# Prompt attention: probabilities, unnormalised and split in two, as the weights of the value product

## The chip, the core and the metric

The kernel runs on one core of a Trainium2 chip. The metric is the time of one launch on the device, in microseconds (us); lower is better. Before the change it is 2110.23 us, the median of three runs (2109.89 to 2110.86). Engines are named as the profile names them: PE is the matmul engine (TensorE), PEld its weight loads, DVE the vector engine, ACT the scalar engine, POOL is GpSimd, SP issues the DMAs.

## The reference

One layer of a hybrid decoder: a combined input projection, latent attention on one side and a gated convolution on the other, one output projection, and an MLP. It treats 1040 prompt tokens (16 learned ones and 1024 of the prompt) and 8 sampled sequences of 4 tokens with a paged cache. Only the attention of the prompt among itself matters here: 8 heads, queries and keys of 96 elements, values of 64.

```python
def block(args):
    qblk, i = args
    qpos = i * Q_BLOCK + jnp.arange(Q_BLOCK)
    s = jnp.einsum('bqhd,bkhd->bhqk', qblk, k).astype(jnp.float32) * ATTN_SCALE
    s = jnp.where(kpos[None, :] <= qpos[:, None], s, -jnp.inf)
    p = jax.nn.softmax(s, axis=-1).astype(v.dtype)
    return jnp.einsum('bhqk,bkhd->bqhd', p, v)
```

Everything is fp32. Where the kernel wants fp32 accuracy from the cheaper matmul on rounded fp32 (type F32R in the code), it splits an operand into a rounded high part and the rest, the low part, and adds three products: high by high, high by low, low by high.

## The kernel before

Six stages run one after the other, with a barrier of all engines behind each: inputs, prompt attention, sampled attention, output projection, MLP, stores. Every engine's program is written out by hand, in order, with semaphores between the engines; there is no scheduler. Only the function `prompt_attention` changes.

It works head by head (`head(n, par, ...)`): head 0, a loop over pairs of heads, head 7. A head has nine blocks of 128 queries, t = 0 to 8 (NT = 9). The last one holds only 16 real tokens of the prompt (1040 = 8 * 128 + 16); the 32 sampled tokens and zeros fill it up. Block t attends to keys 0 to (t + 1) * 128, so it has t + 1 key blocks.

- `transpose_unit` (PE), `split_hi` (ACT), `split_lo` (DVE) turn the next head's queries and keys, four blocks at a time, and split them: five units, in steps t = 1 to 5 of the head before, through bank 5.
- `score` (PE) writes the scores of block t + 2 in step t, queries as weights, keys as the moving side, three products of rounded parts; the mask is added by a matmul of bf16.
- `maxima` (DVE) takes the row maxima of block t + 2 and turns their sign; `probabilities` (ACT) computes the exponentials of block t + 1 and their row sums.
- DVE inverts the row sums of block t and scales its probabilities by them, in place (line 1159).
- PE turns the scaled probabilities with fp32 transposes, in jobs of up to four key blocks ("chunks", at most 512 columns) through the one bank 6 (line 1228). ACT copies each chunk to SBUF (`probsT`, line 1106).
- `values` (PE, line 1204) multiplies, in plain fp32, each key block's values (128 keys x 64, the weights) by the turned probabilities (128 keys x 128 queries, the moving side) and adds up over the key blocks in bank 7. The product of a chunk is issued behind the transposes of the next one. Its result is already values by queries, the form that the output projection wants; ACT copies it to `attnT` (line 1087).

So the order on PE in step t is: scores of t + 2, a unit of the next head, chunk 0 of t, values of the last chunk of t - 1, chunk 1 of t, values of chunk 0 of t, and so on. Every engine takes its instructions strictly in this written order. POOL scales each head's queries, keys and values ahead of time.

Of the kernel before, what the change touches and what calls it, by code (L numbers as in the profile page):

```python
# [971 lines left out]
def prompt_attention(g):  # L972
# [10 lines left out]
    pt = [ar.take(f"probsT{i}", [P, 4, P], F32) for i in range(2)]  # L983
# [4 lines left out]
    vh = [ar.take(f"v_head{i}", [P, NT, VH], F32) for i in range(2)]  # L988
# [4 lines left out]
        "ready gain_done q_head_ready k_head_ready v_head_ready unit_transposed unit_hi_done unit_lo_done scored "  # L993
        "maxed biased exped inverted normed p_transposed p_copied pv_done out_copied").split()}
# [4 lines left out]
    UNIT_BANK = 5  # L999

    SCORE_BANK = (0, 1, 2, 0, 3, 0, 3, 0, 2)
    SCORE_FREE = (-1, -1, 0, 1, 0, 4, 5, 6, 7)

    def chunks(t):
        return [(j, min(4, t + 1 - j)) for j in range(0, t + 1, 4)]
# [6 lines left out]

    def score_shape(t):
        pieces = -(-(t + 1) * P // BANK)
        return pieces, (t + 1) * P // pieces

    def scores(t):
        pieces, n = score_shape(t)
        return banks[:, SCORE_BANK[t]:SCORE_BANK[t] + pieces, 0:n]
# [9 lines left out]
    with nc.Block() as block:  # L1029
        @block.gpsimd  # L1030
        def _(pool):
# [7 lines left out]
            def prepare(n, par):  # L1039
                scale = lambda r, c: r[:, :, ds(n, 1)].broadcast_to([P, NT, c])  # L1040
                pool.wait_ge(s["unit_transposed"], LEAD + n * NU)
# [3 lines left out]
                nc.gpsimd.tensor_mul(kh[:, :, NOPE:QK], g.kpe_tok[:, :, :], scale(g.rk, ROPE)).then_inc(s["k_head_ready"], 1)  # L1045
                if not isinstance(n, int) or n > 1:
                    pool.wait_ge(s["pv_done"], LEAD + n * NCH - NCH)
                nc.gpsimd.tensor_mul(vh[par][:, :, :], g.v_tok[:, :, ds(n * VH, VH)],
                                     g.inv_kv[:, 0:NT].unsqueeze(2).broadcast_to([P, NT, VH])).then_inc(s["v_head_ready"], 1)
# [10 lines left out]
        def _(act):  # L1060
            act.sem_inc(s["exped"], LEAD)
            act.sem_inc(s["p_copied"], LEAD)
            act.sem_inc(s["out_copied"], LEAD)
            act.wait_ge(s["gain_done"], 1)

            def split_hi(n, par, u, bank=UNIT_BANK):
                act.wait_ge(s["unit_transposed"], LEAD + n * NU + (u + 1))
                for queries, t, m, place in UNITS[u]:
                    src = banks[0:QK, bank, place * P:(place + m) * P]
                    if queries:  # L1070
                        act.activation(q_hi[par][0:QK, t * P:(t + m) * P], src, ACT.Copy, scale=g.gg[0:QK, :])\
                            .then_inc(s["unit_hi_done"], 1)
                    else:
                        act.copy(k_hi[par][0:QK, t * P:(t + m) * P], src).then_inc(s["unit_hi_done"], 1)

            def probabilities(n, par, t):
                m = (t + 1) * P
                pieces, L = score_shape(t)
                act.wait_ge(s["biased"], n * NT + (t + 1))
                act.wait_ge(s["p_transposed"], LEAD + n * NCH + before(t - 1))  # L1080
                act.activation(probs[(par + t) % 2][:, 0:m].rearrange("p (a b) -> p a b", a=pieces), scores(t), ACT.Exp,
                               bias=nb[:, t:t + 1], scale=SCALE, accum_out=rs[:, t:t + 1]).then_inc(s["exped"], 1)

            def keep_output(n, par, t):
                act.wait_ge(s["pv_done"], LEAD + n * NCH + before(t + 1))
                w = min(P, TP - t * P)
                act.copy(g.attnT[VH * par:VH * par + VH, ds(n // 2, 1), t * P:t * P + w]
                                      .rearrange("p o t -> p (o t)"), banks[0:VH, 7, 0:w]).then_inc(s["out_copied"], 1)

            def head(n, par, first, last):  # L1090
                if first:
                    for u in range(NU):
                        split_hi(0, 0, u, u)
                    probabilities(0, 0, 0)
                c = 0
                for t in range(NT):
                    if t + 1 < NT:
                        probabilities(n, par, t + 1)
                    elif not last:
                        probabilities(n + 1, 1 - par, 0)  # L1100
                    if not last and 1 <= t <= NU:
                        split_hi(n + 1, 1 - par, t - 1)
                    for j, m in chunks(t):
                        act.wait_ge(s["p_transposed"], LEAD + n * NCH + (c + 1))
                        act.wait_ge(s["pv_done"], LEAD + n * NCH + (c - 1))
                        act.copy(pt[(par + c) % 2][:, 0:m, :], banks[:, 6, 0:m * P].rearrange("p (j q) -> p j q", q=P))\
                            .then_inc(s["p_copied"], 1)
                        c += 1
                        if j == 0 and t >= 1:
                            keep_output(n, par, t - 1)  # L1110
                        elif j == 0 and not first:
                            keep_output(n - 1, 1 - par, NT - 1)
                if last:
                    keep_output(n, par, NT - 1)
# [4 lines left out]
        def _(v):  # L1119
            v.sem_inc(s["unit_lo_done"], LEAD)  # L1120
# [3 lines left out]
            def split_lo(n, par, u, bank=UNIT_BANK):  # L1124
                last = u == NU - 1
                v.wait_ge(s["unit_hi_done"], n * (NU + 1) + (u + 1 + last))
# [8 lines left out]
                if last:  # L1135
                    at = TP - (NT - 1) * P
                    nc.vector.tensor_scalar(g.qs[0:QK, ds(n, 1), :].rearrange("p o t -> p (o t)"), banks[0:QK, bank, at:at + NS],
                                            g.gg[0:QK, :], None, ALU.mult).then_inc(s["unit_lo_done"], 1)
                else:
# [1009 lines left out]
```

## Time and profile before

| | |
|---|---|
| median of three runs | 2110.23 us |
| the profiled execution's own time | 2108.73 us |
| its span, first to last instruction | 2107.0 us |
| prompt attention in it | from 335 to 597 us: 262 us |
| of these, PE busy, granted clock | 251.08 us, 0.97 |
| of these, DVE, ACT, POOL busy | 148.13, 154.96, 39.45 us |
| one head in steady state | 31.47 us |

The timeline names each instruction's start, its duration, engine, line, operation, output and inputs, and the shape; "x8" at the end merges eight of a kind in a row. A plain fp32 matmul appears as two records, a matmul on rounded fp32 as one. A matmul's duration holds its way through the array, and matmuls overlap: what one costs is the distance from one start to the next, which for a merged row of x8 is the duration less that of one (0.27 us at 128 columns), divided by 7. A busy PE in the table is therefore not a PE without stalls.

### The profile page before, as it was taken

How to read it: one execution, taken by the hardware profiler on the slowest of the kernel's cores; microseconds unless marked ns; L12 is line 12 of the kernel's file. 1: busy time of each engine (PE TensorE's matmuls, PEld its weight loads, DVE VectorE, ACT ScalarE, POOL GpSimd, SP SyncE). 2: the span in 40 equal slices, each digit the busy share in tenths (PEclk: the TensorE clock that was granted, in tenths of full speed). 3: DMA queues.
4: the chain of work that ended last, by engine and by line, in shares of the span. 5: the costliest groups of instructions: out<-in, count | busy, mean ns of one | idle time of the engine just before them, and what ended most of it. 6: DMA issues, size and time to landing. Idle time of an engine off the chain costs nothing. (4 is left out here: it accounts for less than half of the span.)

```text
span 2107.0 us, 38039 instructions
## 1 busy us (share of the span) xinstructions
PE 2002.8 (95%) x13358; PEld 1877.5 (89%) x13358; DVE 928.2 (44%) x1679; ACT 796.6 (38%) x1702; POOL 428.4 (20%) x391
## 2 busy tenths in 40 slices
PE   6999997999969999999999698899999999999998
PEld 5999985777749999999998496799999999999998
DVE  6125145556536777777777622521222222221222
ACT  5012134656635666666666311311121111212121
POOL 3233133111010000010000323331222222231221
PEclk7999998999979999999999598899999999999999
DMA  6122000000022222222222111020202011120202
GB/s 213 50 64 63 10 19 9 1 1 0 0 71 63 77 74 73 70 75 73 74 69 107 40 40 29 22 61 26 75 15 65 25 55 50 30 61 24 75 15 97
DMA packets 180599, 108.42 MB, mean 51 GB/s; under 512 B 52132, under 2 KB 177154, under 8 KB 180276
## 3 DMA queue, kind: packets, MB, share of 16 engines
q1 hardware_dynamic: 180358, 107.21, 17.7%
q8 instruction: 44, 0.72, 0.1%
q10 hardware_dynamic: 174, 0.30, 0.1%
q14 instruction: 23, 0.19, 0.0%
HBM read 97.47 MB, written 10.00 MB: 51 GB/s over the span
## 5 line engine op out<-in xcount | busy, mean ns | idle before, releaser
L1750 PE MATMUL banks<-comb_hi,pageT_hi 128*128 128x272 f32 x1024 | 234.3, 310 | 0.0
L1640 DVE TENSOR_REDUCE k_sums<-k_sq 128x8 f32<-128x512 f32 x256 | 174.4, 681 | 92.3 <-ACT k_sq L1462 92.3
L1750 PE MATMUL banks<-comb_hi,pageT_lo 128*128 128x272 f32 x1024 | 212.5, 289 | 0.0
L1750 PE MATMUL banks<-comb_lo,pageT_hi 128*128 128x272 f32 x1024 | 212.2, 289 | 0.0
L1462 ACT ACTIVATE k_sq<-banks 128x512 f32<-128x512 f32 x256 | 152.0, 594 | 142.4 <-PE banks L1750 139.4
L2045 DVE TENSOR_TENSOR xT<-xT,banks 128x1074 f32<-128x1074 f32 x64 | 81.5, 1274 | 277.4 <-PE banks L244 277.4
L2035 DVE TENSOR_TENSOR relu_squared<-relu 128x1074 f32<-128x1074 f32 x32 | 40.9, 1278 | 305.2 <-ACT relu L1949 305.2
L1949 ACT ACTIVATE relu<-banks 128x1074 f32<-128x1074 f32 x32 | 34.3, 1071 | 360.3 <-PE banks L244 351.9
L244 PE MATMUL banks<-a_hi,w_down_hi 128*128 128x358 f32 x768 | 168.2, 327 | 0.0
L244 PE MATMUL banks<-a_hi,w_down_lo 128*128 128x358 f32 x768 | 167.7, 326 | 0.0
L244 PE MATMUL banks<-a_lo,w_down_hi 128*128 128x358 f32 x768 | 167.6, 326 | 0.0
L233 POOL TENSOR_TENSOR w_down_lo<-w_down_raw,w_down_hi 128x512 fp32r<-128x512 f32 x64 | 94.7, 1479 | 348.0 <-ACT w_down_hi L229 348.0
L1750 PEld LDWEIGHTS banks<-comb_lo,pageT_hi 128*128 128x128 f32 x1024 | 161.8, 189 | 0.0
L1750 PEld LDWEIGHTS banks<-comb_hi,pageT_lo 128*128 128x128 f32 x1024 | 161.0, 190 | 0.0
L1750 PEld LDWEIGHTS banks<-comb_hi,pageT_hi 128*128 128x128 f32 x1024 | 158.1, 191 | 0.0
L244 PE MATMUL banks<-hf_hi,w_up_lo 128*128 128x358 f32 x720 | 157.5, 327 | 0.0
L244 PE MATMUL banks<-hf_hi,w_up_hi 128*128 128x358 f32 x720 | 157.0, 326 | 0.3 <-POOL w_up_lo L233 0.3
L244 PE MATMUL banks<-hf_lo,w_up_hi 128*128 128x358 f32 x720 | 157.1, 326 | 0.0
L244 PEld LDWEIGHTS banks<-a_hi,w_down_hi 128*128 128x128 f32 x768 | 133.3, 189 | 0.0
L244 PEld LDWEIGHTS banks<-a_hi,w_down_lo 128*128 128x128 f32 x768 | 132.8, 189 | 0.0
L244 PEld LDWEIGHTS banks<-a_lo,w_down_hi 128*128 128x128 f32 x768 | 131.6, 189 | 0.0
L229 ACT CAST w_down_hi<-w_down_raw 128x512 fp32r<-128x512 f32 x64 | 39.5, 617 | 237.4 <-PE banks L244 237.4
(371 smaller groups left out, 4044.3 us busy)
## 6 DMA issues: line engine op xcount, KB each, us to landing
page_latents<-in_cache_kv_latent SPq DMA_DIRECT2D x256, 128.0 KB, 2.1
w_up_raw<-in_w_up SPq DMA_DIRECT2D x32, 512.0 KB, 4.2
w_down_raw<-in_w_down SPq DMA_DIRECT2D x64, 256.0 KB, 2.8
w_in_raw<-in_w_in SPq DMA_DIRECT2D x17, 512.0 KB, 3.8
x_spill<-xT SPq DMA_DIRECT2D x1, 4296.0 KB, 13.9
xT<-x_spill SPq DMA_DIRECT2D x1, 4296.0 KB, 12.8
page_ropes<-in_cache_k_rope SPq DMA_DIRECT2D x256, 16.0 KB, 1.8
w_o_raw<-in_w_o SPq DMA_DIRECT2D x8, 512.0 KB, 4.2
```

The source lines that it names most:

```text
L229: act.copy(self.hi[s][:, :, :], self.raw[s][:, :, :]).then_inc(self.hi_done[s], 1)
L233: nc.gpsimd.tensor_sub(self.lo[s][:, :, :], self.raw[s][:, :, :], self.hi[s][:, :, :].bitcast(F32)).then_inc(self.lo_done[s], 1)
L244: mm = pe.matmul(out[:, b, 0:TB], w[s][:, k, :], x(k)[:, b * TB:(b + 1) * TB], start=k == 0 and a == 0, stop=k == self.K - 1 and a == 2)
L1462: act.activation(sq[j % 2][:, :].rearrange("p (a c) -> p a c", a=2), kn[:, :, 0:WK], ACT.Square)\
L1640: nc.vector.tensor_reduce(ksum[par][:, j, :], sq[j % 2][:, :].rearrange("p (h c) -> p h c", h=H), AX_X, ALU.add)\
L1750: mm = pe.matmul(banks[:, 2 * (j % 2) + half, 0:WC], x[j % AHEAD][:, k, :], w[par][:, k, half, :], start=k == 0 and a == 0, stop=k == KL - ...
L1949: act.activation(relu[:, f % 2, :].rearrange("p (b t) -> p b t", b=NBLK), banks[:, 3 * (f % 2):3 * (f % 2) + 3, 0:TB], ACT.Relu)\
L2035: nc.vector.tensor_mul(full[:, s, :], relu[:, s, :], relu[:, s, :]).then_inc(sq_done, 1)
L2045: nc.vector.tensor_add(x, x, banks[:, 3 * s:3 * s + 3, 0:TB]).then_inc(down.evacuated[s], 1)
```

## The change

The exponentials are no longer scaled. PE turns them as they are; ACT writes their rounded high part (`probsT_hi`) and DVE the rest (`probsT_lo`). The value product changes sides: the turned probabilities (128 keys x 128 queries) are the weights, the values the moving side. POOL splits the values too, into one tile of 128 columns, 64 high and 64 low. Each key block takes two matmuls on rounded fp32: the high probabilities by all 128 columns, the low probabilities by the 64 high ones. The result has queries on the partitions and two halves; ACT scales the low half by the inverse row sum (`scale_low`), DVE scales the high half and adds the low one (`keep_output`), into `out_tokens`. Behind the last head, PE turns all of `out_tokens`, 36 transposes in nine groups, and ACT and DVE copy the groups to `attnT` in turns.

The units and the chunks share two banks, 5 and 6, in turns: a job may start when the last but one is split. Block 8 works on its 16 real rows only, turns its nine key blocks in one job of 16 columns each, and the values of that job are issued behind the scores of block 2 of the next head.

```diff
-    pt = [ar.take(f"probsT{i}", [P, 4, P], F32) for i in range(2)]
+    pt_hi, pt_lo = ([ar.take(f"{n}{i}", [P, 4, P], F32R) for i in range(2)] for n in ("probsT_hi", "probsT_lo"))
...
-    vh = [ar.take(f"v_head{i}", [P, NT, VH], F32) for i in range(2)]
+    vf = ar.take("v_head", [P, NT, VH], F32)
+    vh = [ar.take(f"v_head_split{i}", [P, NT, 2 * VH], F32R) for i in range(2)]
+    part = [ar.take(f"out_low{i}", [P, VH], F32) for i in range(2)]
+    out_tok = ar.take("out_tokens", [P, NT, AW], F32)
...
-        return [(j, min(4, t + 1 - j)) for j in range(0, t + 1, 4)]
+        return [(j, min(4, t + 1 - j)) for j in range(0, t + 1, 4)] if t < LAST else [(0, NT)]
...
+    def job_bank(n, par, at):
+        return 5 + (at + par * NJ) % 2
...
     def score_shape(t):
+        if t == LAST:
+            return 3, 352
...
             def prepare(n, par):
...
+                nc.gpsimd.tensor_mul(vh[par][:, :, 0:VH], g.v_tok[:, :, ds(n * VH, VH)],
+                                     g.inv_kv[:, 0:NT].unsqueeze(2).broadcast_to([P, NT, VH])).then_inc(s["v_high"], 1)
...
+                nc.gpsimd.tensor_sub(vh[par][:, :, VH:2 * VH], vf[:, :, :], vh[par][:, :, 0:VH].bitcast(F32))\
+                    .then_inc(s["v_head_ready"], 1)
...
+            def scale_low(n, t, scaled):
+
                 act.wait_ge(s["pv_done"], LEAD + n * NCH + before(t + 1))
...
+                act.activation(part[scaled % 2][0:rows(t), :], banks[0:rows(t), OUT_BANK, VH:2 * VH], ACT.Copy,
+                               scale=ri[0:rows(t), t:t + 1]).then_inc(s["out_scaled"], 1)
...
                     for j, m in chunks(t):
-                        act.wait_ge(s["p_transposed"], LEAD + n * NCH + (c + 1))
+                        job = job_of_chunk(n, t, c, last)
+                        act.wait_ge(s["turned"], LEAD + job + 1)
                         act.wait_ge(s["pv_done"], LEAD + n * NCH + (c - 1))
-                        act.copy(pt[(par + c) % 2][:, 0:m, :], banks[:, 6, 0:m * P].rearrange("p (j q) -> p j q", q=P))\
-                            .then_inc(s["p_copied"], 1)
+                        act.copy(split_keys(pt_hi[(par + c) % 2], t, m), turned_keys(job_bank(n, par, in_head(t, c, last)), t, m))\
+                            .then_inc(s["hi_done"], 1)
...
+            def keep_output(n, t, scaled):
+                v.wait_ge(s["out_scaled"], LEAD + n * NT + (t + 1))
+                nc.vector.scalar_tensor_tensor(out_tok[0:rows(t), t, ds(n * VH, VH)], banks[0:rows(t), OUT_BANK, 0:VH], ri[0:rows(t), t:t + 1],
+                                               part[scaled % 2][0:rows(t), :], ALU.mult, ALU.add).then_inc(s["out_done"], 1)
...
                 for t in range(NT):
                     v.wait_ge(s["exped"], LEAD + n * NT + (t + 1))
-                    nc.vector.reciprocal(ri[:, t:t + 1], rs[:, t:t + 1]).then_inc(s["inverted"], 1)
-                    v.wait_ge(s["inverted"], n * NT + (t + 1))
-                    pr = probs[(par + t) % 2][:, 0:(t + 1) * P]
-                    nc.vector.tensor_scalar(pr, pr, ri[:, t:t + 1], None, ALU.mult).then_inc(s["normed"], 1)
+                    nc.vector.reciprocal(ri[0:rows(t), t:t + 1], rs[0:rows(t), t:t + 1]).then_inc(s["inverted"], 1)
                     if t + 2 < NT:
-                        maxima(n, par, t + 2)
+                        maxima(n, t + 2)
...
+                    for j, m in chunks(t):
+                        v.wait_ge(s["hi_done"], LEAD + job_of_chunk(n, t, c, last) + 1)
+                        nc.vector.tensor_sub(split_keys(pt_lo[(par + c) % 2], t, m),
+                                             turned_keys(job_bank(n, par, in_head(t, c, last)), t, m),
+                                             split_keys(pt_hi[(par + c) % 2], t, m).bitcast(F32)).then_inc(s["split"], 1)
+                        c += 1
+                        if j == 0 and t >= 1:
+                            keep_output(n, t - 1, par + t - 1)
...
-                pe.wait_ge(s["p_copied"], LEAD + n * NCH + (c + 1))
+                pe.wait_ge(s["split"], LEAD + job_of_chunk(n, t, c, last) + 1)
                 if j == 0:
-                    pe.wait_ge(s["out_copied"], LEAD + n * NT + t)
+                    pe.wait_ge(s["out_done"], LEAD + n * NT + t)
+                hi, lo = split_keys(pt_hi[(par + c) % 2], t, m), split_keys(pt_lo[(par + c) % 2], t, m)
                 for x in range(m):
-                    mm = pe.matmul(banks[0:VH, 7, 0:P], vh[par][:, j + x, :], pt[(par + c) % 2][:, x, :],
-                                   start=j + x == 0, stop=j + x == t)
+                    k = slice(0, rows(j + x))
+                    pe.matmul(banks[0:rows(t), OUT_BANK, 0:2 * VH], hi[k, x, :], vh[par][k, j + x, :], start=j + x == 0, stop=False)
+                    mm = pe.matmul(banks[0:rows(t), OUT_BANK, 0:VH], lo[k, x, :], vh[par][k, j + x, 0:VH], start=False, stop=j + x == t)
                 mm.then_inc(s["pv_done"], 1)
...
                     for j, m in chunks(t):
-                        pe.wait_ge(s["p_copied"], LEAD + n * NCH + c)
+                        job, bank = job_of_chunk(n, t, c, last), job_bank(n, par, in_head(t, c, last))
+                        pe.wait_ge(s["split"], LEAD + job - 1)
+                        if t == LAST:
+                            values(*behind)
+                            behind = None
...
+                if last:
+                    values(*behind)
+                    for t in range(NT):
+                        pe.wait_ge(s["out_done"], LEAD + n * NT + (t + 1))
...
+                        for k in range(AW // P):
+                            mm = pe.transpose(banks[:, t % 4, k * P:k * P + rows(t)], out_tok[0:rows(t), t, k * P:(k + 1) * P],
+                                              ident[0:rows(t), 0:rows(t)])
+                        mm.then_inc(s["out_turned"], 1)
```

How the written order moves, at two places. In the rows a name's number tells buffers apart; REGISTER_ALU and ISA rows prepare a wait's value in the loop over heads. First DVE, from block 5's step on, before: the sums inverted, the probabilities scaled, then the maxima of block 7 and the last unit's split.

```order
L1156 RECIPROCAL row_inv<-row_sum 128x1
L1159 TENSOR_SCALAR probs_2934<-probs_2934,row_inv 128x768
L1144 TENSOR_REDUCE row_max<-banks 128x1
L1146 TENSOR_SCALAR neg_max<-row_max 128x1
L1126 REGISTER_ALU
L1131 SCALAR_TENSOR_TENSOR q_lo_2918<-banks,qk_gain,q_hi_2916 96x128
L1134 TENSOR_TENSOR k_lo_2922<-banks,k_hi_2920 96x128
L1137 ISA
L1137 TENSOR_SCALAR q_sampled<-banks,qk_gain 96x32
L1155 REGISTER_ALU
L1156 RECIPROCAL row_inv<-row_sum 128x1
L1159 TENSOR_SCALAR probs_2935<-probs_2935,row_inv 128x896
```

The same step now, from the maxima of block 7 on.

```order
L1202 TENSOR_REDUCE row_max<-banks 128x1
L1204 TENSOR_SCALAR neg_max<-row_max 128x1
L1183 REGISTER_ALU
L1185 REGISTER_ALU
L1190 SCALAR_TENSOR_TENSOR q_lo_2918<-banks,qk_gain,q_hi_2916 96x128
L1193 TENSOR_TENSOR k_lo_2922<-banks,k_hi_2920 96x128
L1196 ISA
L1196 TENSOR_SCALAR q_sampled<-banks,qk_gain 96x32
L1229 REGISTER_ALU
L1230 TENSOR_TENSOR probsT_lo_2927<-banks,probsT_hi_2925 128x512
L1208 ISA
L1208 SCALAR_TENSOR_TENSOR out_tokens<-banks,row_inv,out_low_2942 128x64
```

The scaling is gone, and behind the maxima and the unit's split stand two new steps that PE waits for: the low parts of block 5's chunk of 512 columns (`probsT_lo`) and the sum of an output block (`out_tokens`).

Second PE, at the end of a head, before: block 8's three chunks, each followed by the values of the one ahead of it, then the scores of the next head's block 2.

```order
L1204 MATMUL banks<-probsT_2924,v_head_2937 64x128 x4
L1226 REGISTER_ALU
L1228 MATMUL banks<-ident,probs_2935 128x128 x4
L1202 REGISTER_ALU
L1204 MATMUL banks<-probsT_2925,v_head_2937 64x128 x4
L1226 REGISTER_ALU
L1228 MATMUL banks<-ident,probs_2935 128x128
L1204 MATMUL banks<-probsT_2924,v_head_2937 64x128 x4
L1200 REGISTER_ALU
L1204 MATMUL banks<-probsT_2925,v_head_2937 64x128
L1190 REGISTER_ALU
L1195 MATMUL banks<-k_hi_2920,q_hi_2916 128x384
```

The same place now: block 8's one job, then the scores of the next head's block 2, its first chunk, and the first of block 8's value products.

```order
L1318 MATMUL banks<-ident,probs_2937 128x16 x8
L1318 MATMUL banks<-ident,probs_2937 16x16
L1269 REGISTER_ALU
L1276 MATMUL banks<-k_hi_2920,q_hi_2916 128x384
L1276 MATMUL banks<-k_lo_2922,q_hi_2916 128x384
L1274 MATMUL banks<-causal_mask,ident_bf_2929 128x128
L1276 MATMUL banks<-k_hi_2920,q_lo_2918 128x384
L1307 REGISTER_ALU
L1312 ISA
L1318 MATMUL banks<-ident,probs_2936 128x128
L1281 REGISTER_ALU
L1287 MATMUL banks<-v_head_split_2940,probsT_hi_2925 16x128
```

Three chunks became one with 16 columns a key block, and its values moved behind the scores and the first chunk of the next head.

## Rows read from the trace of the kernel before

**Rows 1.** Windows view, one steady head: us, busy of PE, PEld, DVE, ACT, POOL; clock.
```profile
core 0: us, PE busy (x) PEld busy (x) DVE busy (x) ACT busy (x) POOL busy (x), PEclk, DMA share, GB/s
425.88:457.35 31.47, 30.77 (x210) 23.80 (x207) 18.74 (x44) 19.33 (x49) 4.95 (x5) 1.00 0.00 1
```

**Rows 2.** Groups by shape, attention stage: busy us, mean ns, idle before and its enders.
```profile
L1228 PE MATMUL banks<-ident,probs 128*128 128x128 f32 x360 | 62.7, 283 | 3.7 <-ACT probsT L1106 2.5 <-DVE probs L1159 0.4
L1134 DVE TENSOR_TENSOR k_lo<-banks,k_hi 96x512 fp32r<-96x512 f32 x16 | 11.0, 685 | 0.2 <-ACT k_hi L1074 0.2
```

**Rows 3.** Timeline, PE, starts around blocks 4 to 8: start, duration, instruction, tiles, count.
```profile
425.29 0.27 PE L1182 MATMUL banks<-ident,q_head 128*96 128x128 f32 x1
...
428.17 0.44 PE L1195 MATMUL banks<-k_hi,q_hi 96*128 96x384 f32 x1
...
429.99 0.60 PE L1228 MATMUL banks<-ident,probs 128*128 128x128 f32 x4
...
431.27 0.55 PE L1228 MATMUL banks<-ident,probs 128*128 128x128 f32 x3
...
432.76 0.33 PE L1195 MATMUL banks<-k_hi,q_hi 96*128 96x128 f32 x1
...
433.23 0.62 PE L1228 MATMUL banks<-ident,probs 128*128 128x128 f32 x4
...
436.18 0.38 PE L1195 MATMUL banks<-k_hi,q_hi 96*128 96x256 f32 x1
...
436.77 0.60 PE L1228 MATMUL banks<-ident,probs 128*128 128x128 f32 x4
...
441.42 0.44 PE L1195 MATMUL banks<-k_hi,q_hi 96*128 96x384 f32 x1
...
451.55 0.60 PE L1182 MATMUL banks<-ident,k_head 128*96 128x128 f32 x4
...
455.12 0.50 PE L1195 MATMUL banks<-k_hi,q_hi 96*128 96x512 f32 x1
```

**Rows 4.** Timeline, DVE, the maxima and what starts behind them.
```profile
425.49 1.23 DVE L1144 TENSOR_REDUCE row_max<-banks 128x1 f32<-128x1024 f32 x1 [2.57 <-PE banks L1195]
...
427.47 0.15 DVE L1156 RECIPROCAL row_inv<-row_sum 128x1 f32<-128x1 f32 x1
...
430.19 1.36 DVE L1144 TENSOR_REDUCE row_max<-banks 128x1 f32<-128x1152 f32 x1 [1.05 <-PE banks L1195]
...
431.58 0.15 DVE L1146 TENSOR_SCALAR neg_max<-row_max 128x1 f32<-128x1 f32 x1
...
451.75 1.09 DVE L1144 TENSOR_REDUCE row_max<-banks 128x1 f32<-128x896 f32 x1 [0.80 <-PE banks L1195]
...
453.58 0.15 DVE L1156 RECIPROCAL row_inv<-row_sum 128x1 f32<-128x1 f32 x1
```

**Rows 5.** Timeline, ACT, one copy of turned probabilities.
```profile
430.63 0.58 ACT L1106 COPY probsT<-banks 128x512 f32<-128x512 f32 x1 [1.89 <-PE banks L1228]
```

**Rows 6.** Timeline, PE and PEld: prices of matmuls and of weight loads.
```profile
263.00 2.36 PEld L894 LDWEIGHTS banks<-ones,lora_squares 128*128 128x128 f32 x20
...
432.93 0.28 PE L1195 MATMUL banks<-k_lo,q_hi 96*128 96x128 f32 x1
...
433.04 0.23 PE L1194 MATMUL banks<-causal_mask,ident_bf 128*128 128x128 bf16 x1
...
433.08 0.31 PE L1195 MATMUL banks<-k_hi,q_lo 96*128 96x128 f32 x1
...
435.18 1.08 PE L1204 MATMUL banks<-probsT,v_head 128*64 128x128 f32 x8
```

**Rows 7.** Groups by shape, weight loads of rounded fp32 in the sampled stage.
```profile
L1750 PEld LDWEIGHTS banks<-comb_hi,pageT_lo 128*128 128x128 f32 x1024 | 161.0, 190 | 0.0
```

**Rows 8.** Timeline, the end of the attention stage.
```profile
594.80 1.31 PE L1204 MATMUL banks<-probsT,v_head 128*64 128x128 f32 x10
...
596.14 0.16 ACT L1087 COPY attnT<-banks 64x16 f32<-64x16 f32 x1 [0.97 <-PE banks L1204]
```

More of the change, by code:

```diff
@@ L1079, in probabilities @@
+                    done.then_inc(s["hi_done"] if i == len(UNITS[u]) - 1 else s["unit_hi"], 1)
+            def probabilities(n, t):
+                m = score_shape(t)[0] * score_shape(t)[1]
                 act.wait_ge(s["biased"], n * NT + (t + 1))
[L1080 to L1082 removed]
@@ L1092, in head @@
                     for u in range(NU):
[L1093 to L1094 removed]
+                        unit_high(0, u, u, u)
+                    parity["par"] = 0
+                    probabilities(0, 0)
                 c = 0
@@ L1097, in head @@
                     if t + 1 < NT:
-                        probabilities(n, par, t + 1)
-                    elif not last:
-                        probabilities(n + 1, 1 - par, 0)
-                    if not last and 1 <= t <= NU:
-                        split_hi(n + 1, 1 - par, t - 1)
+                        parity["par"] = par
+                        if t >= 1:
+                            act.wait_ge(s["turned"], LEAD + job_of_chunk(n, t - 1, before(t) - 1, last) + 1)
+                        elif not first:
+                            act.wait_ge(s["turned"], LEAD + job_of_chunk(n - 1, LAST, NCH - 1, False) + 1)
@@ L1103, in head @@
+                        probabilities(n, t + 1)
+                    elif not last:
+                        parity["par"] = 1 - par
+                        act.wait_ge(s["turned"], LEAD + job_of_chunk(n, t - 1, before(t) - 1, last) + 1)
+                        probabilities(n + 1, 0)
+                    if not last and UNIT_AT(t) is not None:
+                        u = UNIT_AT(t)
+                        unit_high(1 - par, u, job_bank(n, par, before(t) + u), job_of_unit(n, u))
                     for j, m in chunks(t):
-                        act.wait_ge(s["p_transposed"], LEAD + n * NCH + (c + 1))
+                        job = job_of_chunk(n, t, c, last)
+                        act.wait_ge(s["turned"], LEAD + job + 1)
@@ L1164, in head @@
-                    if not last and 1 <= t <= NU:
-                        split_lo(n + 1, 1 - par, t - 1)
+                        maxima(n + 1, t + 2 - NT)
+                    if not last and UNIT_AT(t) is not None:
+                        u = UNIT_AT(t)
+                        unit_low(n + 1, 1 - par, u, job_bank(n, par, before(t) + u), job_of_unit(n, u))
+                    for j, m in chunks(t):
[6 more added lines that the diff above has]
+                            keep_output(n, t - 1, par + t - 1)
+                        elif j == 0 and not first:
+                            keep_output(n - 1, LAST, 1 - par + LAST)
@@ L1167, in _ @@
+                if last:
+                    keep_output(n, LAST, par + LAST)
+                    for t in range(1, NT, 2):
+                        v.wait_ge(s["out_turned"], t + 1)
+                        nc.vector.tensor_copy(g.attnT[:, :, t * P:t * P + rows(t)],
+                                              banks[:, t % 4, :].rearrange("p (k q) -> p k q", q=P)[:, :, 0:rows(t)])\
+                            .then_inc(s["out_copied_dve"], 1)
             heads(v, head)
```

166 lines of the change are left out of this document (98 added, 68 removed).

## Prediction

> **What bounds the kernel now.** I read the windows view first, for the stage and one head in it, then the timeline of that head on PE and on DVE side by side, then the waits and single prices. The change lives in the prompt attention alone, 262 of 2107 us. In a steady head PE is busy for 30.77 of 31.47 us while DVE and ACT are busy for 18.74 and 19.33 and POOL for 4.95 [rows 1]. So PE bounds the stage, and the clock is full (1.00) all through the head. But a busy PE holds short waits: the matmuls' ends reach over the next start. What counts is the distance between starts. The reader is to see in [rows 3] the five stretches between the end of one block's scores and the start of the next block's scores, in which the value path runs. I name them by the block t whose probabilities are turned there: t=4 from 451.55 to 455.12, 3.57 us; t=5 from 425.29 to 428.17, 2.88; t=6 from 429.99 to 432.76, 2.77; t=7 from 433.23 to 436.18, 2.95; t=8 from 436.77 to 441.42, 4.65. Wherever PE must wait for another engine in the new order, the stretch grows, however cheap its matmuls became.
>
> **Prices.** A turn of one key block costs (0.60 - 0.27) / 3 = 0.11 us [rows 3]. A value product before: eight records, four products, start 435.18, next scores 436.18, so 1.00 us for four, of which (1.08 - 0.27) / 7 = 0.116 a record or 0.232 a product, and 0.07 us for the change of group [rows 3, 6]. From the end of a turn to ACT's copy pass 0.04 us, the copy of 512 columns takes 0.58, and PE starts 0.06 us behind it (430.59, 430.63, 431.21, 431.27) [rows 3, 5]. The new split on DVE is the operation that splits keys now: 512 columns out of PSUM, 0.69 us [rows 2].
>
> The new product takes two matmuls per key block. The first, 128 rounded columns behind a fresh load of 128 weight columns, is of the shape of block 0's scores: from 432.93 to 433.04, 0.11 us [rows 6]. The second, 64 columns, is in no row. Its load is: twenty loads of 128 fp32 columns for matmuls of only 2 columns came (2.36 - 0.19) / 19 = 0.114 us apart, so a load that nothing hides sets the pace at 0.114 [rows 6], and a load of rounded fp32 has the same duration, 190 ns against 0.19 us [rows 6, 7]. I take 0.11 + 0.112 = 0.222 us a pair. Bounds: 0.15 if the second matmul costs what the mask's bf16 matmul does (433.04 to 433.08, 0.04), 0.34 if no load runs ahead of its matmul, as for the first of a group (432.76 to 432.93, 0.17) [rows 3, 6]; the stream of twenty is the nearest row, since there too each matmul brings its load. So 0.232 becomes 0.222: the weights are twice as wide now, and a product still loads twice.
>
> [...]
>
> **The steps, one steady head.** DVE takes its work in the written order, and the new split of chunk 0 of block t stands behind the maxima of block t + 2, which wait for the scores that PE has just finished. Behind PE's wait for that split stand the values, then the next scores, so all of it is on the path. Time counts from the start of the stretch.
> - t=4: DVE starts the maxima at 0.20, and what stands behind them and the unit's split starts at 453.58 - 451.55 = 2.03 [rows 3, 4]. There the split goes: 2.03 + 0.69 + 0.06 = 2.78 until PE goes on, then four pairs, 4 x 0.222 + 0.07 = 0.96: 3.74 against 3.57, +0.17.
> - t=5: 427.47 - 425.29 = 2.18 until the unit's parts are done [rows 3, 4], + 0.69 + 0.06 + 0.96 = 3.89 against 2.88, +1.01. This is the largest wait: PE has only 1.2 us of other work there.
> - t=6: the maxima of block 8 end with the sign change at 431.58 - 429.99 = 1.59 [rows 3, 4]; 96 columns fewer take 0.10 off (1.36 against 1.23 us for 128), the sign change 0.15: 1.64 + 0.69 + 0.06 + 0.96 = 3.35 against 2.77, +0.58.
> - t=7: the maxima are short; turn and copy decide: 0.64 + 0.58 + 0.04 + 0.69 + 0.06 + 0.96 = 2.97 against 2.95, +0.02.
> - t=8: four pairs 0.96 and one turn of nine key blocks with 16 columns. No row has that shape; between 0.04 and 0.11 I take 0.06 each, 0.61 in all. Block 8's nine pairs have 16 weight columns, so the matmuls decide: 0.11 for 128 columns and half of it for 64, 9 x 0.17 + 0.07 = 1.60 (bounds 0.08 and 0.22 a pair). They run behind the next scores, which hide their split. 3.17 against 4.65, -1.48.
> - Scores of block 8: 32 of 384 columns less, 1.82 us (428.17 to 429.99) x 32 / 384 = -0.15. Blocks 0 to 2: six pairs, -0.06.
>
> Sum: +0.09 us a head. PE's work falls by about 2 us and the waits give it back. The scaling that goes was not on the path: PE waited 0.4 us for it in the whole stage [rows 2]. DVE gains some 4 us a head (6.9 of splits by [rows 2]'s price, 2 of outputs, less 5 of scaling) and stays under 23 of 31. ACT loses work. POOL's two new multiplications and a subtraction of under 1.2 us each fit: it is busy for 5 of 31 us. If DVE's idle time were gone, each further 0.1 us in front of a split would cost PE 0.1.
>
> **Head 7 and the end.** Without units, t=4 and t=5 lose 0.3 us of their penalty together, and the 0.4 us wait for the scaling goes, but no next scores hide the split of block 8, about 0.8 us, nor that of block 7's second chunk, 0.3: together +0.3 us. Then the new tail: eight groups of four turns at 0.44 + 0.07 and one at 0.24, 4.32 us, and a last copy, some 0.45. Before, only a copy of 0.16 us followed the last product (596.14 to 596.30, 0.34 us behind the ten records from 594.80 at 0.116 each) [rows 8]. Net +4.4, since nothing runs beside it: the next stage stands behind a barrier. ACT and DVE need 0.58 and 0.69 us for every second group, less than PE's 1.02, so the copies do not bound it.
>
> Total: 7 x 0.09 + 0.3 + 4.4 = +5.3 us. Against the profiled execution's own 2108.73 us that is 2114.0; the median of the runs lies 1.5 us above that execution, and so I predict 2110.2 + 5.3 = 2115.5, rounded to 2116 us.
>
> **Rivals.**
> A. PE becomes really cheaper: the second matmul hides its load or both do. At 0.15 a pair a head loses 36 x 0.072 = 2.6 us on PE, 2.0 of it where values are on the path, and block 8's pairs at 0.08 another 0.8: 8 x 2.8 = 22, so 2094 us (faster). For it: the sampled stage's loads vanish behind 272 columns. Against it: the 0.114 of [rows 6], and 64 columns are short. Chance 0.13.
> B. Only block 8 is cheaper than I put it (0.08 a pair, turns at 0.04): -1.0 a head, 2108 us, no change. For it: the mask's 0.04. Against: 433.04 - 432.93 = 0.11 for 128 rounded columns. Chance 0.22.
> C. The new loop through ACT and DVE adds waits that I do not see: DVE stops at the output's sum until ACT has scaled the low half, which waits for values on PE, which wait for DVE. It decides as soon as ACT's scaling comes later than DVE's first split in t=4 to t=7; a small ACT step, two handovers and a small DVE step cost 0.16 + 0.04 + 0.06 + 0.15 = 0.41 us [rows 3 to 5, 8], in four steps 1.6 a head, 13 in all: 2129 us. For it: steps t=4 to t=6 are already bound by DVE. Against: the values it needs end 1 to 2 us earlier in each of those steps. Chance 0.17.
> D. That the change does not do what it says is the forecast itself in part: rounded fp32 does not make the product cheaper, for the loads bind it.
>
> **Numbers.** Forecast 0.48, A 0.13, B 0.22, C 0.17. Faster or slower is meant by over 0.2%, 4.2 us, about what runs of this kernel can tell from no change: below 2106.0 or above 2114.5. The forecast's own range is 2111 to 2121, a third of it within 0.2%. Faster: A and a fifth of B, 0.18. Same: the rest of B and a quarter of the forecast, 0.30. Slower: 0.52. For 8 in 10 I take 2101 to 2130; it leaves out most of A, the upper part of C, and the far end of a pair's price (0.34, 8 x 36 x 0.12 = 34 us more), to which I give hardly any chance.
>
> **What would show it.** In the new trace: pairs of the value product 0.22 us apart or not; PE idle in t=5 by over 1 us with DVE's split as the releaser, and by about 0.5 in t=6; block 8's nine pairs in some 1.6 us; heads 31.5 us apart; and 4 to 5 us of transposes alone at the stage's end. Heads under 30 us, or pairs under 0.15, would make the prediction wrong on the fast side; heads over 32.5 with idle time on PE in t=1 to t=3 or t=7 on the other.

## The result, and the profile after

The changed kernel takes 2187.31 us (median of four runs, 2184.97 to 2197.98) against 2110.06 before: 1.0377 times as long, 95% interval 1.0343 to 1.0412. The forecast was 2116 us, with a range from 2101 to 2130. It is wrong. All times here are medians; one launch of the run before_short_block8, which took 5120 us, is left out of its median.

The profiled execution took 2184.97 us. From its page, the granted clock in 40 slices of some 55 us, in tenths of the full clock:

```profile
PEclk8999996666665999999999779799999999999999
```

The windows view, cut at the stage's ends and then by heads 2 and 3 (busy us of PE, PEld, DVE, ACT, POOL, then the clock):

```profile
0.00:335.00 335.00, 308.74 (x1826) 297.23 (x1826) 114.65 (x130) 89.71 (x130) 103.45 (x100) 0.96 0.23 67
335.00:674.00 339.00, 311.56 (x1692) 262.41 (x1692) 171.40 (x454) 147.80 (x374) 57.68 (x58) 0.66 0.00 1
674.00:2183.20 1509.20, 1444.91 (x9876) 1388.75 (x9876) 666.13 (x1204) 552.41 (x1187) 285.81 (x252) 0.96 0.20 57
...
402.43:442.63 40.20, 37.45 (x209) 31.42 (x209) 20.99 (x57) 17.76 (x47) 7.09 (x6) 0.67 0.00 1
442.63:484.21 41.58, 39.47 (x208) 33.07 (x208) 21.15 (x57) 18.05 (x47) 7.09 (x6) 0.62 0.00 0
```

All of the loss lies in the prompt attention: 339 us instead of 262, the rest within 1 us. A head takes 40 to 42 us instead of 31.47 [rows 1]. PE is busy for 0.93 to 0.95 of a head, against 0.98 before, but its clock is 0.62 to 0.67 in these two heads, not 1.00. Of the stage's 339 single microseconds the windows view puts 96 at a clock of 1.00, 216 at 0.50, 27 in between and none below, so such a mean is a mixture of full and half clock. Some of one head:

```profile
456.00:457.00 1.00, 1.00 (x8) 1.00 (x6) 0.21 (x1) 0.59 (x1) 0.00 (x0) 0.50 0.00 0
...
473.00:474.00 1.00, 1.00 (x8) 0.88 (x7) 0.85 (x3) 1.00 (x4) 0.00 (x0) 1.00 0.00 0
...
479.00:480.00 1.00, 0.44 (x3) 0.14 (x1) 1.00 (x3) 0.53 (x3) 0.00 (x0) 1.00 0.00 0
480.00:481.00 1.00, 0.70 (x7) 0.73 (x7) 0.45 (x3) 1.00 (x3) 0.00 (x0) 1.00 0.00 0
481.00:482.00 1.00, 1.00 (x8) 0.87 (x8) 0.00 (x0) 0.06 (x1) 0.00 (x0) 1.00 0.00 0
482.00:483.00 1.00, 1.00 (x5) 0.47 (x3) 0.00 (x0) 0.00 (x0) 0.00 (x0) 0.55 0.00 0
```

The reader is to see two things. PE can be busy for a whole microsecond at half the clock (456: busy 1.00, clock 0.50), and it is so for most of this head; the full clock comes back only from 472 to 482. And the fall at 482 follows value products with short waits around them. The timeline of PE there, with the idle time and its releaser in brackets, and one pair of products at either clock:

```profile
445.10 0.45 PE L1287 MATMUL banks<-v_head_split,probsT_hi 128*128 128x128 f32 x1 [0.19 <-DVE out_tokens L1208]
445.34 0.36 PE L1288 MATMUL banks<-v_head_split,probsT_lo 128*128 128x64 f32 x1
445.52 0.45 PE L1287 MATMUL banks<-v_head_split,probsT_hi 128*128 128x128 f32 x1
...
472.63 0.30 PE L1287 MATMUL banks<-v_head_split,probsT_hi 128*128 128x128 f32 x1
472.77 0.25 PE L1288 MATMUL banks<-v_head_split,probsT_lo 128*128 128x64 f32 x1
472.85 0.31 PE L1287 MATMUL banks<-v_head_split,probsT_hi 128*128 128x128 f32 x1
...
479.42 0.33 PE L1318 MATMUL banks<-ident,probs 128*128 128x128 f32 x1 [0.32 <-DVE k_lo L1193]
480.30 0.30 PE L1287 MATMUL banks<-v_head_split,probsT_hi 128*128 128x128 f32 x1 [0.55 <-DVE out_tokens L1208]
```

A pair takes 0.22 us at the full clock (472.63 to 472.85), as forecast, and 0.42 at half of it. PE's waits in the head from 442.63:

```profile
PE banks L1287 <- DVE out_tokens L1208: 1.1, 3, 0.6
PE banks L1318 <- DVE q_sampled L1196: 0.7, 1, 0.7
PE banks L1318 <- DVE k_lo L1193: 0.3, 1, 0.3
```

They are 2.1 of 41.58 us, and by [rows 1] the kernel before stands idle for 0.7 of 31.47 us. So at most 1.4 of the lost 10 us are waits; the rest is work at the lower clock. What lowers the clock was open: the new waits, or the new products.

**Theory 1, the stream.** A pair streams 192 columns in 0.22 us, paced by its two weight loads, which start 0.11 us apart (PEld, from 472.60). While PE's row says busy, little moves through it, and the clock goes by that. **Theory 2, the waits.** The waits for DVE, up to 1.5 us, drop the clock, whatever the products are.

### The profile page after: what moved, and what is told of

It reads as the page before. It is cut to its first block and busy times, and to the rows that moved or that the text cites. A ratio compares the mean times of both kernels' runs of the same rounds, so it can differ in the third digit from the quotient of the medians.

```text
span 2183.2 us, 38384 instructions
## 1 busy us (share of the span) xinstructions
PE 2065.2 (95%) x13394; PEld 1948.4 (89%) x13394; DVE 952.2 (44%) x1787; ACT 789.9 (36%) x1691; POOL 446.9 (20%) x407
## 5 line engine op out<-in xcount | busy, mean ns | idle before, releaser
L1287 PE MATMUL banks<-v_head_split,probsT_hi 128*128 128x128 f32 (+1 forms) x360 | 115.1, 369 | 13.6 <-DVE out_tokens L1208 13.6
```

The lines of the kernel that those rows point to most:

```text
L1287: pe.matmul(banks[0:rows(t), OUT_BANK, 0:2 * VH], hi[k, x, :], vh[par][k, j + x, :], start=j + x == 0, stop=False)
```

## Experiments

**More columns in the second product** (wide_low).

```diff
-  mm = pe.matmul(banks[0:rows(t), OUT_BANK, 0:VH], lo[k, x, :], vh[par][k, j + x, 0:VH], ...)
+  mm = pe.matmul(banks[0:rows(t), OUT_BANK, 0:2 * VH], lo[k, x, :], vh[par][k, j + x, :], ...)
```

> The changed kernel, but the second product of each key block streams all 128 value columns (it adds the tiny low-times-low products, 64 columns more) instead of 64. Same two weight loads per key block, same waits. Theory 1 (the value products stream too few columns for the time that their weight loads take, and the clock stays at its lower level though TensorE is never idle): the granted clock of the prompt stage rises well above 0.65 and the time falls to 2110 to 2165. Theory 2 (the waits of about 1 us for VectorE in blocks 4 to 6 drop the clock): clock stays at 0.62 to 0.68, time 2180 to 2195.

2155.44 us, 1.0218 (1.0197 to 1.0238): 32 us of the 77 come back. Three heads in a row, by the windows view:

```profile
432.34:473.90 41.56, 38.47 (x210) 32.36 (x208) 21.14 (x57) 18.05 (x47) 7.07 (x6) 0.67 0.00 0
473.90:507.84 33.94, 29.79 (x211) 24.64 (x208) 20.74 (x57) 17.93 (x47) 7.09 (x7) 0.90 0.00 0
507.84:545.54 37.70, 33.98 (x210) 28.15 (x208) 21.05 (x57) 18.01 (x47) 7.07 (x6) 0.77 0.00 0
```

More work on PE, with loads and order unchanged, and a shorter time: that speaks for theory 1. PE's waits did not shrink: from 400 to 560 us they are 14.9 us, against 9.7 in the changed kernel. Heads of one program differ by 8 us with the clock alone.

**The split ahead of the maxima** (split_first). VectorE's `unit_low`, then the first chunk's split, then `maxima(t + 2)`, then the output sum.

```diff
+  (in the loop over chunks, behind the split of a chunk:)
+  if j == 0 and t + 2 < NT:
+      maxima(n, t + 2)
+  elif j == 0 and not last:
+      maxima(n + 1, t + 2 - NT)
   (these lines go from their old place, ahead of the unit's split)
```

> The changed kernel, but VectorE does a block's unit split and the split of its first chunk before the row maxima of the block two ahead. Streams and loads of TensorE unchanged, waits at the split in blocks 4 to 6 mostly gone. Theory 2 (waits): the clock stays near 1.00 through the heads, a head takes 31 to 32 us, time 2100 to 2115. Theory 1 (thin stream): the clock stays near 0.65, a head 38 to 41 us, time 2165 to 2185.

2259.55 us, 1.0711 (1.0690 to 1.0733). It did not do what it was made for. The output sum of the block before now stood behind the maxima, and PE's next products wait for that sum. Waits from 335 to 720 us, most of the stage:

```profile
PE banks L1287 <- DVE out_tokens L1208: 50.6, 44, 2.3
```

That is 50.6 us where the changed kernel has 13.6 in its whole stage. So the run does not decide between the two theories (the stage's clock is 0.62, against 0.66); it says that the sum stands on the path, which the forecast had missed.

**Waits put into the kernel before** (before_late_scaling).

```diff
+  if t < 7:
       nc.vector.tensor_scalar(pr, pr, ri[:, t:t + 1], None, ALU.mult).then_inc(s["normed"], 1)
   ... maxima(n, par, t + 2) ...
+  if t >= 7: (the same scaling here)
```

> The kernel before, but for query blocks 7 and 8 VectorE scales the probabilities only after the row maxima of the block two ahead, so that TensorE waits 1 to 2 us twice a head before it can turn them; its products and their streams are those of before. Theory 2 (waits of 1 us drop the clock): the clock of the stage falls below 0.8 and the time goes to 2160 or above. Theory 1 (thin stream): the clock stays at 0.95 or above, the waits cost only themselves, 1.5 to 3 us in a head, time 2122 to 2135.

2137.00 us, 1.0130 (1.0109 to 1.0152). A head takes 34.69 us, 3.2 more than [rows 1]; its waits, then its windows row:

```profile
PE banks L1231 <- DVE probs L1166: 2.8, 2, 1.5
PE banks L1231 <- ACT probsT L1106: 0.3, 1, 0.3
```

```profile
399.36:434.05 34.69, 31.17 (x210) 23.87 (x207) 18.40 (x44) 19.00 (x49) 4.95 (x4) 1.00 0.01 1
```

A head has 3.4 us of waits, up to 1.5 us each, against 2.1 in the changed kernel's, a little more than I had put. The clock stays at 1.00; in eight heads it falls once (553.5). With the old products the waits cost little more than themselves (eight heads of 3.2 us are 26 of the 27 us): theory 2 falls as a cause that is enough by itself. The time is just above the 2122 to 2135 of theory 1.

**Block 8 cut to 16 queries, alone** (before_short_block8): `chunks`, `score_shape`, `rows` as in the change, and plain fp32 products with 16 moving columns.

```diff
-  mm = pe.matmul(banks[0:VH, 7, 0:P], vh[par][:, j + x, :], pt[(par + c) % 2][:, x, :], ...)
+  mm = pe.matmul(banks[0:VH, 7, 0:rows(t)], vh[par][k, j + x, :], copied_keys(pt[(par + c) % 2], t, m)[k, x, :], ...)
```

> The kernel before with one part of the change alone: query block 8 is cut to its 16 real queries (scores 352 wide in 16 rows, nine turns of 16 columns, nine plain fp32 products of 16 moving columns). Values, scaling and banks stay as before. By the trace of before block 8 has nine products at 0.232 us and nine turns at 0.11 us a head; cut to 16 columns they should take about half or less. Both theories, if the short products of under 2 us a head do not touch the clock: 1.5 to 2.5 us less a head, 2090 to 2100, clock at 1.00. Theory 1 in a strong form: the thin stretch of block 8 drops the clock, and time goes above 2110.

2121.25 us, 1.0060 (1.0040 to 1.0080): slower, though it only leaves out work on empty rows. I had expected 2090 to 2100, and only the strong form of theory 1 had 2110 or more. Timeline and windows around one block 8:

```profile
441.12 0.69 PE L1246 MATMUL banks<-ident,probs 16*128 16x16 f32 x9
442.33 0.87 PE L1218 MATMUL banks<-probsT,v_head 128*64 128x16 f32 x12 [0.52 <-ACT attnT L1099]
```

```profile
442.00:443.00 1.00, 0.67 (x12) 0.67 (x12) 0.00 (x0) 0.78 (x4) 0.00 (x0) 1.00 0.00 0
443.00:444.00 1.00, 1.00 (x12) 0.91 (x10) 0.00 (x0) 0.07 (x1) 0.18 (x1) 0.87 0.08 16
444.00:445.00 1.00, 1.00 (x6) 0.66 (x4) 0.00 (x0) 0.00 (x0) 0.97 (x1) 0.50 0.00 0
```

The clock falls behind the nine short turns and nine short products, once a head, and stays at half for 3.4 to 6.8 us (13.7 us the last time), though wide scores follow at once.

**The same with 128 columns again** (before_block8_wide).

```diff
-  pe.matmul(banks[0:VH, 7, 0:rows(t)], ..., copied_keys(pt[(par + c) % 2], t, m)[k, x, :], ...)
+  pe.matmul(banks[0:VH, 7, 0:P], ..., (the flat buffer)[:, x * rows(t):x * rows(t) + P], ...)
```

> The kernel before with block 8's scores and turns cut to its 16 queries as before_short_block8, but its nine products stream 128 columns again (the other 112 columns are neighbouring or left-over keys, and nothing reads their results). If the clock fell after block 8 because its products were thin, it stays at 1.00 now and the time is 2095 to 2108; if the short turns and the waits at them did it, it falls once a head as in before_short_block8, 2115 to 2125.

2109.95 us, 1.0004 (0.9994 to 1.0015). The turns are as short as before and the wait ahead of the products is the same 0.52 us. Only the products' columns differ, and the clock stays full. The time is just above the 2095 to 2108 I had for it.

```profile
438.92 0.69 PE L1247 MATMUL banks<-ident,probs 16*128 16x16 f32 x9
440.13 2.32 PE L1219 MATMUL banks<-probsT,v_head 128*64 128x128 f32 x18 [0.52 <-ACT attnT L1099]
```

```profile
427.06:458.31 31.25, 30.02 (x210) 22.71 (x207) 18.53 (x44) 17.96 (x47) 4.95 (x5) 1.00 0.00 1
```

Nine products with 112 columns that nobody reads made the launch 11 us faster than nine without. This pair and the next are the cleanest evidence for theory 1.

**256 columns in every product of blocks 0 to 7** (filled); in block 8 both products stream 128.

```diff
+  twice = 2 if t < LAST else 1
+  out = banks[0:rows(t), OUT_BANK, 0:twice * 2 * VH].rearrange("p (a b) -> p a b", a=twice)
+  moving = vh[par][k, j + x, :].unsqueeze(1).broadcast_to([rows(j + x), twice, 2 * VH])
+  pe.matmul(out, hi[k, x, :], moving, start=j + x == 0, stop=False)
+  mm = pe.matmul(out, lo[k, x, :], moving, start=False, stop=j + x == t)
```

> The changed kernel, but in query blocks 0 to 7 both products of a key block stream 256 columns (the 128 value columns twice over, into 256 columns of the bank, of which only the first 128 are read; it also adds low times low). Loads, waits and all other engines as in the changed kernel; since a pair there takes 0.222 us for 192 columns and is bound by its two loads, 256 columns each should cost nothing or up to 0.02 us a pair. Theory 1 (too few columns stream): the granted clock of the prompt stage is back at 0.9 or more, a head takes 32 to 34 us, time 2105 to 2130, near the 2116 forecast. The rival (the waits for VectorE hold the clock down, alone or as much as the stream): clock 0.65 to 0.8 and time 2150 or above.

2126.84 us, 1.0081 (1.0064 to 1.0097): 60 of the 77 us come back, from columns of which the added ones are not read. Two heads, then a pair and the wait in block 5's stretch, from the timeline:

```profile
426.43:458.48 32.05, 27.50 (x210) 22.96 (x208) 20.72 (x57) 17.79 (x47) 7.10 (x6) 1.00 0.00 1
458.48:492.07 33.59, 28.95 (x211) 23.61 (x208) 20.60 (x57) 17.82 (x47) 7.09 (x7) 0.95 0.00 0
```

```profile
428.23 0.44 PE L1321 MATMUL banks<-ident,probs 128*128 128x128 f32 x2 [1.35 <-DVE q_sampled L1196]
429.11 0.36 PE L1290 MATMUL banks<-v_head_split,probsT_hi 128*128 128x256 f32 x1 [0.44 <-DVE out_tokens L1208]
...
429.66 0.28 PE L1290 MATMUL banks<-v_head_split,probsT_hi 128*128 128x256 f32 x1
429.78 0.28 PE L1291 MATMUL banks<-v_head_split,probsT_lo 128*128 128x256 f32 x1
429.90 0.28 PE L1290 MATMUL banks<-v_head_split,probsT_hi 128*128 128x256 f32 x1
```

The waits are longer than in the changed kernel (4.4 us in the head from 426.43; 21.3 us from 400 to 560, against 9.7) and yet the clock is 1.00 or, where it falls once behind block 5 (in four heads, one of them that from 458.48), 0.95. A pair takes 0.24 us (429.66 to 429.90) instead of 0.22, so 320 columns more cost 0.02.

**Shorter row maxima, thin products kept** (short_max): the row maxima of blocks 2 to 8 over every fourth key, which was meant to take the waits away.

```diff
-  nc.vector.tensor_reduce(mx[...], scores(t), ...)
+  nc.vector.tensor_reduce(mx[...], scores(t)[:, :, 0::4] if t >= 2 else scores(t), ...)
```

> The changed kernel, but for query blocks 2 to 8 VectorE takes the row maximum over every fourth key only (the shift of the exponentials is then that of a quarter of the keys). This takes about three quarters off the maxima of 1.0 to 1.6 us that stand ahead of VectorE's unit split and probability split, and with them most of TensorE's waits; the products stay thin. Theory 1 (stream): the clock stays below 0.8 in the stage, time 2150 to 2180. Rival (waits): clock 0.95 or more, a head 30.5 to 31.5 us, time 2095 to 2115.

2185.16 us, 1.0355 (1.0330 to 1.0381): as the changed kernel. I had put theory 1 at 2150 to 2180; its clock came true (0.68 in the row below), the size did not. But the edit did not do what it was made for. Below the row stand PE's waits from 400 to 560 us:

```profile
475.03:514.45 39.42, 37.02 (x211) 31.12 (x210) 16.94 (x56) 17.84 (x47) 7.09 (x6) 0.68 0.00 0
```

```profile
PE banks L1287 <- DVE out_tokens L1208: 6.2, 12, 0.9
PE banks L1318 <- DVE q_sampled L1196: 2.4, 4, 0.9
```

They are 8.6 us, against 9.7 in the same stretch of the changed kernel. So this run still has thin products and short waits together, and does not test the rival.

**Both** (filled_short_max). 

> Both edits: 256 columns in each product and row maxima over every fourth key. Theory 1 and the rival agree: waits gone and stream full, clock 0.95 or more in the stage, a head 30 to 31.5 us, time 2090 to 2112. If it stays above 2140 both theories miss something, the likeliest being block 8's short turns and products, which dropped the clock once a head when they alone were put into the kernel before.

2112.75 us, 1.0014 (1.0004 to 1.0023), a head 31.08 us at a clock of 1.00: just above the upper end of what was expected. Here too most of the waits stayed (18.4 us from 400 to 560, against 21.3 in filled), but the clock no longer falls in the heads. Eight heads shorter by 0.97 us, and four falls less at some 1.5 us each (33.59 against 32.05), make up the 14 us to filled.

**Another order** (scores_between; the filled products). The scores of the block two ahead go between the first chunk's turn and its products; VectorE splits first, sums, then takes the maxima.

```diff
   (PE, behind values(*behind) in the loop over chunks:)
+  if j == 0 and t + 2 < NT:
+      score(n, par, t + 2, None)
   (DVE, behind the split and the output sum:)
+  if j == 0 and t + 2 < NT:
+      maxima(n, t + 2)
   (both go from their old place, ahead of the unit)
```

> The filled kernel (256 columns in each product of blocks 0 to 7) with another order in a stretch: TensorE turns the next head's unit and the block's first chunk and does the products left over before it computes the scores of the block two ahead, so that these lie between the first chunk's turn and its products; VectorE does the unit's split, the first chunk's split and the output sum ahead of the row maxima. If the waits for the split are only a matter of what lies between, the 4 us of waits in a head of the filled kernel fall below 1.5 us, the clock (now without gaps of over 1 us) stays at 0.95 or more, a head takes 28 to 30 us and the time is 2080 to 2105, below both kernels. If the loop of scores, maxima, exponentials and turns is what sets the stretch (theory C of the forecast), the waits come back at the turns, a head stays at 31 to 33 us, time 2110 to 2130.

> The same order, and row maxima over every fourth key. If VectorE's maxima are what is late in that order, this is 1 to 2 us a head faster than with the full maxima; if not, the two are alike within 5 us. In both cases 2075 to 2105.

> The same order with full maxima, but the products of the changed kernel (128 and 64 columns). If thin products alone hold the clock down, waits or none: clock below 0.8 in the stage, 2150 us or more. If gaps and thin products must come together: clock 0.95 or more and 2070 to 2100.

With full maxima 2133.32 us, 1.0113 (1.0096 to 1.0130): above both ranges. In kind the second came true: the waits of the head from 432.38 (33.68 us) moved to turns, those of the next head's units:

```profile
PE banks L1261 <- DVE q_lo L1190: 2.3, 2, 1.2
PE banks L1290 <- DVE out_tokens L1208: 1.6, 4, 0.6
PE banks L1261 <- DVE k_lo L1193: 0.6, 1, 0.6
```

With the short maxima 2105.39 us, 0.9979 (0.9969 to 0.9989), 30.47 us a head, at the edge of the 2075 to 2105; the 28 us between the two runs are more than the 8 to 16 us I had for it. With thin products 2178.58 us, 1.0328 (1.0287 to 1.0369): 45 us slower than the filled one of the same order, and as expected for thin products, 2150 us or more and a clock below 0.8. The stage's clock is 0.73; it is 0.66 up to 448.91 and higher in the two heads behind that:

```profile
448.91:485.32 36.41, 32.08 (x209) 26.53 (x208) 20.79 (x56) 17.85 (x47) 7.09 (x7) 0.84 0.00 0
```

PE still waits here (4.3 us in this head), so thin products without waits were not put to the test. The stage of the changed kernel has 0.66: the order of the work, waits included, may have a part in how often the clock falls where the products are thin. The runs do not separate it.

**ScalarE in the new order too** (exp_after_copy): the exponentials of the next block behind the unit split, the copy and the output scaling; full maxima, filled products.

```diff
-  (first in the loop over blocks:)  probabilities(n, t + 1)
+  (behind the first chunk's copy and scale_low:)  probabilities(n, t + 1)
```

> The order of scores_between with full row maxima and 256 columns in each product, and ScalarE too in another order: a block's unit split, the copy of its first chunk and the output scaling come before the exponentials of the next block, which until now stood ahead of them. In scores_between TensorE waited some 5 us a head, most of it for unit and chunk splits that stood behind exponentials, which stood behind the row maxima. If that order is what is late, the waits halve, the clock stays at 1.00, a head takes 30 to 31.5 us (33.7 before this edit), and the time is 2095 to 2115, at or a little below the kernel before. If VectorE's maxima themselves are what is late, the waits move to the turns, a head stays above 32.5 us and the time at 2120 to 2135.

2107.35 us, 0.9986 (0.9977 to 0.9995): 2.7 us faster than the kernel before, with the interval below 1. A head and its waits:

```profile
389.53:419.33 29.80, 27.52 (x207) 22.97 (x207) 21.14 (x58) 17.82 (x47) 7.10 (x6) 1.00 0.01 2
```

```profile
PE banks L1291 <- DVE probsT_lo L1227: 1.2, 3, 0.6
PE banks L1318 <- ACT probs L1119: 0.4, 1, 0.4
```

The waits halve, and a head is 1.67 us shorter than in [rows 1]. Of the 13 us that eight such heads make, the turns at the end take some 5 back; one fall of the clock (a head of 32.40 us) takes 2.6. Some 6 us should be left; 2.7 are measured, and 4.4 between the profiled executions. The rest is not accounted for.

## Why the prediction was wrong, step by step

- **The failed step: the clock.** "So PE bounds the stage, and the clock is full (1.00) all through the head" was read from [rows 1] and carried over to other products without a word. No term, bound or rival let it change. The runs showed 0.62 to 0.67 in a head, 0.66 in the stage. Four heads of the changed kernel take 40.8 us on the mean (402.43 to 565.65); the forecast's head was 31.56. Eight times 9.2 is 74 us, and with the forecast's own +5 that is the measured +77 within 2 us.
- **The pair, 0.222 us: right** at the full clock (0.22). Its loads start 0.11 us apart (472.60, 472.71, 472.82), the pace that [rows 6] had at 0.114. But the price was the wrong thing to stop at: that loads pace a pair means that few columns stream, and the clock went with the columns: 0.66 in the stage with 192 columns a pair, 0.80 with 256 (wide_low, 335 to 639), 0.96 with 512 (filled, 335 to 608.7). At half the clock the pair takes 0.42.
- **The waits in blocks 4 to 6: right in place, too small.** At the full clock (filled) the stretches of t=4 to t=7 took 4.08 (from 452.28), 4.31 (425.82), 3.63 (431.80) and 3.41 us (435.79) against 3.74, 3.89, 3.35 and 2.97; the four wider pairs behind the split make 0.06 of each. Missing is the output sum: PE may not start the next products until DVE has summed the bank's last output, and that instruction stands behind the split. It is 0.27 us long:

```profile
428.69 0.27 DVE L1208 SCALAR_TENSOR_TENSOR out_tokens<-banks,row_inv,out_low 128x64 f32 x1
```

Rival C looked at the same sum, but for another wait: of DVE for ACT's scaling of the low half, at 0.41 us. DVE does not wait here; ACT's part has ended at 427.55, a microsecond earlier.
- **Block 8's pairs: 1.28 us (filled, 128 columns in each product) against 1.60;** its nine turns 0.62 against 0.61 (440.73 to 441.35).
- **The head's sum held, in part by luck.** 32.05 us in the filled kernel against 31.56; up to 36 x 0.015 = 0.5 of it are the wider pairs (at the full clock 0.238 us on the mean, 0.223 in the changed kernel). The waits were some 1.3 us under-priced; blocks 0 to 3 (some 0.4 us), the scores between the stretches (0.35) and block 8 (0.2) came out shorter than the forecast has them and gave most of it back.
- **The end: right in kind.** From 666.95 to the end of the last copy 5.69 us, against 4.77 forecast; its clock was 0.75.

```profile
666.95 5.45 PE L1335 MATMUL banks<-ident,out_tokens 128*128 128x128 f32 x36
```

```profile
672.43 0.21 ACT L1169 COPY attnT<-banks 128x64 f32<-128x64 f32 x1 [0.20 <-PE banks L1335]
```

- **Rivals.** A and B asked whether PE gets cheaper, C whether waits are added. With the clock mostly held (filled) the launch takes 2127 us, inside the range, though 11 us above the forecast. None of the three looked at the clock.

Shown is that most of the loss needs the thin products: with the waits as long or longer, more columns bring the clock back (from 0.66 in the stage to 0.80 in wide_low and 0.96 in filled; from 0.88 in before_short_block8 to 0.97 in before_block8_wide, 335 to 597). Left open is whether thin products lower the clock without any wait, for no run has them so: short_max and thin_scores_between, which were meant to, kept theirs. The changed kernel's fall at 482 follows waits of 0.32 and 0.55 us, and the one at 472 in short_max a wait of 0.55. With the full stream of filled the clock fell behind longer ones, of 1.35 and 0.44 us in block 5, in four heads; in the head from 426.43 it stayed full behind the same two.

## What to carry to other kernels

When a change replaces matmuls by others, ask not only what one costs but how much it streams while its weights load: here the stage whose pairs stream 192 columns behind two loads ran at a clock of 0.66, and other work in it about doubled in price at the half clock (a turn of 128 columns took 0.21 us instead of 0.11 in the row from 483.79). Check the clock of the stage before looking for waits; where it is low while PE is busy, widen the moving side, read or not, as far as the price allows (here 320 columns more in a pair cost 0.015 us on the mean), and see whether the clock comes back. And after an edit that is meant to take a wait away, read the waits again before drawing on its time. And a wait behind a queue is as long as all that stands ahead of it, the small sums included.

## What the runs showed of the hardware that was not expected

- PE at half the full clock while its busy row is 1.00 (456 to 457, clock 0.50), for most of a 41.58 us head (clock 0.62). Waits of up to 1.5 us between the old products, in before_late_scaling, left the clock at 1.00 but for one fall in eight heads.
- Less work, more time: nine products cut from 128 to 16 columns made the launch 11 us slower, through 3.4 to 6.8 us (once 13.7) at half clock in a head.
- Pairs of 256 columns each take 0.238 us on the mean behind 128-column loads (filled), pairs of 128 and 64 take 0.223 (the changed kernel): 320 columns more add 0.015 us. At half the clock the pair of 128 and 64 takes 0.42, and its loads start 0.21 us apart (445.24, 445.45, 445.66) instead of 0.11: what paces it slows down with the clock.
- Nine turns of 16 columns take 0.62 us (filled, 440.73 to 441.35), 0.07 each, against 0.11 for 128 columns.
